# Score products in sets of three levels in a hybrid decoder step (GLA, HGRN2, convolution, pooling)

## The reference, cut to what matters

```python
h = _rmsnorm(x, norm_pre[l]); c = _split_cols(h @ w_in[l])
# groups A and C, per head of 64 channels, in blocks:
b = jnp.cumsum(gc, axis=2)
decay = jnp.exp(jnp.where(causal, b[:, :, :, None, :] - b[:, :, None, :, :], -jnp.inf))
scores = jnp.einsum('bhtd,bhsd,bhtsd->bhts', qc, kc, decay)
o = einsum('bhts,bhsv->bhtv', scores, vc) + einsum('bhtd,bhdv->bhtv', qc * jnp.exp(b), S)
S = exp(b_last)[..., None] * S + einsum('bhsd,bhsv->bhdv', kc * jnp.exp(b_last[:, :, None, :] - b), vc)
...
x = x + _rmsnorm(concatenate([o_a, o_b, o_c, o_d]) @ w_out[l], norm_post[l])
```

## Time and profile before

| what | value |
|---|---|
| median of 3 runs | 1050.87 us |
| span of the profiled execution, first to last instruction | 1048.4 us |
| what lies around the span (median less span) | 2.5 us |
| TensorE busy | 1005.1 us, 11780 matmuls |
| VectorE, ScalarE, GpSimd busy | 643.7, 434.0, 382.3 us |
| one tile of the loop, from a_k to the next a_k | 118.5 us |

### The profile page before, as it was taken

How to read it: one execution, slowest core, us unless ns; L and a number is a source line. 1 busy time by engine, 2 the same in 40 slices (tenths; PEclk the granted TensorE clock), 3 DMA queues, 4 the chain that set the end, 5 groups by cost and what they waited for, 6 DMA issues and landing times.

```text
span 1048.4 us, 27477 instructions
## 1 busy us (share of the span) xinstructions
PE 1005.1 (96%) x11780; PEld 749.1 (71%) x11780; DVE 643.7 (61%) x1356; ACT 434.0 (41%) x861; POOL 382.3 (36%) x526
## 2 busy tenths in 40 slices
PE   2998799999999999999999999999999999999997
PEld 2857477865887668865787668865787668866683
DVE  4997678645745567446745467446746477346564
ACT  6874444532534334432444334432434325233323
POOL 1434432174305640174304640164304650156300
PEclk9997699999999999999999999999999999999999
DMA  8720341001100011001100011001100011000011
GB/s 313 265 105 4 108 145 47 22 2 42 62 22 1 2 62 61 1 2 42 62 21 2 1 62 62 1 2 41 62 22 1 3 61 42 2 2 27 17 65 43
DMA packets 16187, 49.96 MB, mean 48 GB/s; under 512 B 2449, under 2 KB 3259, under 8 KB 16059
## 3 DMA queue, kind: packets, MB, share of 16 engines
q1 hardware_dynamic: 16067, 48.21, 13.2%
HBM read 38.44 MB, written 9.86 MB: 46 GB/s over the span
## 4 chain that ended last, share of the span: by engine, by line
PE 68%; DVE 21%; ACT 6%; issue 3%; DMA 1%; SPq 1%; POOL 0%; DVEq 0%; ACTq 0%
PE pj L676 30%; PE op L892 15%; PE pj L695 7%; PE sc L769 5%; DVE A L1896 4%; DVE w_lo L1789 2%; DVE X L2097 1%; DVE X L2090 1%; DVE X L2099 1%; PE op L738 1%; PE m L874 1%; PE m L826 1%; PE sc L912 1%; DVE A L1908 1%; PE op L912 1%
## 5 line engine op out<-in xcount | busy, mean ns | idle before, releaser
L676 PE MATMUL pj<-h_hi,w_hi 128*128 128x256 f16 (+1 forms) x1728 | 211.7, 266 | 1.0 <-DVE K L1840 0.5
L676 PE MATMUL pj<-h_lo,w_hi 128*128 128x256 f16 (+1 forms) x1728 | 210.2, 265 | 0.0
L676 PE MATMUL pj<-h_hi,w_lo 128*128 128x256 f16 (+1 forms) x1728 | 209.0, 264 | 0.0
L1896 DVE COPY_PREDICATED A<-cu,sc 64x128 f32<-64x128 uint8 x384 | 132.0, 344 | 114.3 <-PE sc L769 107.8
L501 POOL TENSOR_TENSOR G<-B 128x256 f32<-128x256 f32 x112 | 79.0, 705 | 294.5 <-DVE B L1831 171.2
L676 PEld LDWEIGHTS pj<-h_hi,w_hi 128*128 128x128 f16 x1728 | 152.3, 99 | 28.6 <-issue 4.4
L676 PEld LDWEIGHTS pj<-h_lo,w_hi 128*128 128x128 f16 x1728 | 158.7, 99 | 18.0
L676 PEld LDWEIGHTS pj<-h_hi,w_lo 128*128 128x128 f16 x1728 | 158.2, 99 | 17.5
L512 POOL TENSOR_TENSOR G<-G,Q 128x256 f32<-128x256 f32 x112 | 86.6, 773 | 117.4 <-issue 70.0
L1327 ACT ACTIVATE G<-G 128x512 f32<-128x512 f32 x112 | 69.1, 621 | 77.7 <-POOL G L502 77.6
L513 POOL TENSOR_TENSOR G<-G,K 128x256 f32<-128x256 f32 x112 | 92.6, 827 | 0.0
(11 more groups left out here) (284 smaller groups left out, 1402.2 us busy)
## 6 DMA issues: line engine op xcount, KB each, us to landing
xin<-in_x_prompt SPq DMA_DIRECT2D x17, 512.0 KB, 3.5
wo_hi<-in_w_units SPq DMA_DIRECT2D x16, 512.0 KB, 5.4
xres<-in_x_prompt SPq DMA_DIRECT2D x15, 512.0 KB, 3.6
out_y_prompt<-xres SPq DMA_DIRECT2D x14, 512.0 KB, 2.6
wo_lo<-in_w_units SPq DMA_DIRECT2D x12, 512.0 KB, 5.0
xres<-in_w_out SPq DMA_DIRECT2D x8, 256.0 KB, 3.2
gpost<-in_w_out SPq DMA_DIRECT2D x8, 256.0 KB, 4.2
m_hi<-in_state_gla SPq DMA_DIRECT2D x1, 512.0 KB, 8.5
```

The costliest lines, as they stand in the source:

```text
L676: m = pe.matmul(b[:, j * T:(j + 1) * T], w[:, k, col + 128 * j:col + 128 * j + 128], h[:, k, :], start=(n == 0 and k == 0), stop=(n == 2 a ...
L1896: m = dve.copy_predicated(out, mk.unsqueeze(1).broadcast_to([64, 4, 32 // h, h]), half(SC[hh], u)[:, 0:128].rearrange("p (q b w) -> p q b ...
```

## The change

1. From tile 2 on (`FIRST_SETS = 2`), the levels are grouped in `SETS`: 0 to 2, 3 to 5, and 6 with DIAG. The products of a set go to columns 0, 128 and 256 of SC and are issued one after the other; only the first of them waits for the copies of the set before. The copies wait for the last product of the set.
2. TensorE's list: six sets per tile in place of sixteen single products; `attend` and `updates` of a branch follow each other; both of branch 1 come after `b_b`; `recall(i, 1)` comes after `b_z`; `head_sums(i, 1)` between the halves of `c_z`.
3. GpSimd, ScalarE and VectorE get new orders; tile 8 uses the loop on these three, and on TensorE a list like that of the loop.
4. The fills of `pj` in tile 8 are in the order of the other tiles.

No computation is left out, and the number of instructions that compute stays the same.

```diff
+SETS = ((0, 1, 2), (3, 4, 5), (6, DIAG))
+FIRST_SETS = 2
...
+def set_of(i, lv):
+
+    if i < FIRST_SETS:
+        return (lv,)
+    return next(g for g in SETS if lv in g)
...
-            for i in range(2, NT):
+            for i in range(2, NT + 1):
                 for br in range(2):
-                    for lv in range(3):
+                    for lv in (0, 1, 2):
                         exponents(i, br, lv)
-                    factors(i, br, 0)
                     if br == 1:
                         key_product(i, 0)
-                    factors(i, br, 1)
-                    exponents(i, br, 3)
-                    for lv in range(2, 7):
+                    for lv in (0, 1, 2):
                         factors(i, br, lv)
-                        if lv < 5:
-                            exponents(i, br, lv + 2)
+                    for lv in (3, 4, 5):
+                        exponents(i, br, lv)
+                    for lv in (3, 4, 5):
+                        factors(i, br, lv)
                     key_exponents(i, br)
+                    exponents(i, br, 6)
+                    factors(i, br, 6)
                 key_product(i, 1)
...
         def scores(i, br, lv):
             T, NC, C = dims(i)
-            n = at_score(i, br, lv)
-            if n or i:
+            n, at_col = at_score(i, br, lv), CH * set_of(i, lv).index(lv)
+            if (n or i) and at_col == 0:
                 pe.wait_ge(*at("am", i, 2 * n))
...
-                                    col = (2 * c + j) * 32
+                                    col = at_col + (2 * c + j) * 32
...
+        def score_set(i, br, n):
+
+            for lv in SETS[n]:
+                scores(i, br, lv)
...
                 proj(i, "c_f")
                 proj(i, "a_q")
                 proj(i, "a_k")
-                values_proj(i, 0, (0,))
-                scores(i, 0, 0)
-                values_proj(i, 0, (1,))
-                scores(i, 0, 1)
+                values_proj(i, 0)
                 values_proj(i, 1, (0,))
-                scores(i, 0, 2)
+                score_set(i, 0, 0)
                 values_proj(i, 1, (1,))
-                scores(i, 0, 3)
-                proj(i, "c_q", (0,))
-                scores(i, 0, 4)
-                proj(i, "c_q", (1,))
-                scores(i, 0, 5)
+                proj(i, "c_q")
                 out_product(i - 1, 0, 0)
-                scores(i, 0, 6)
+                score_set(i, 0, 1)
                 out_product(i - 1, 0, 1)
-                scores(i, 0, DIAG)
                 proj(i, "d_v", (0,))
-                attend(i, 0)
+                score_set(i, 0, 2)
                 proj(i, "d_v", (1,))
                 transpose_keys(i, 0)
-                scores(i, 1, 0)
                 out_product(i - 1, 1, 0)
+                attend(i, 0)
                 updates(i, 0)
-                scores(i, 1, 1)
                 out_product(i - 1, 1, 1)
-                scores(i, 1, 2)
+                score_set(i, 1, 0)
                 recall(i, 0)
-                scores(i, 1, 3)
                 pool_product(i)
-                proj(i, "d_z", (0,))
-                scores(i, 1, 4)
-                proj(i, "d_z", (1,))
+                proj(i, "d_z")
                 head_sums(i, 0)
-                scores(i, 1, 5)
                 proj(i, "a_z", (0,))
-                scores(i, 1, 6)
+                score_set(i, 1, 1)
                 proj(i, "a_z", (1,))
-                if i < NT:
-                    transpose_x(i + 1, 0)
-                scores(i, 1, DIAG)
+                transpose_x(i + 1, 0)
                 proj(i, "b_c")
+                score_set(i, 1, 2)
+                proj(i, "b_v")
+                transpose_keys(i, 1)
+                transpose_x(i + 1, 1)
+                proj(i, "b_b")
                 attend(i, 1)
-                transpose_keys(i, 1)
-                proj(i, "b_v")
                 updates(i, 1)
...
-                proj(i, "b_b")
+                low_rank(i + 1)
+                proj(i, "b_z")
                 recall(i, 1)
...
+                log_alpha(i + 1)
+                proj(i, "c_z", (0,))
                 head_sums(i, 1)
-                proj(i, "c_z")
+                proj(i, "c_z", (1,))
...
         def copy_scores(i, br, lv):
             T, NC, C = dims(i)
-            n = at_score(i, br, lv)
+            n, at_col = at_score(i, br, lv), CH * set_of(i, lv).index(lv)
             for hh in range(2):
-                dve.wait_ge(*at("sc", i, 2 * n + hh + 1))
+                if at_col == 0:
+                    dve.wait_ge(*at("sc", i, 2 * at_score(i, br, set_of(i, lv)[-1]) + hh + 1))
+                else:
+                    dve.wait_ge(*at("am", i, 2 * n + hh - 1))
...
```

More of the change, by code:

```diff
@@ L79, in fill_order @@
     fills += [
-        (NT, "c_f"), (NT, "a_q"), (NT, "a_k"), (NT, "vi0"), (NT, "c_q"), (NT, "vi1"), (NT, "d_v"),
-        (NT, "d_z"), (NT, "po"), (NT, "a_z"), (NT, "b_c"), (NT, "b_v"), (NT, "b_b"), (NT, "tails"),
+        (NT, "c_f"), (NT, "a_q"), (NT, "a_k"), (NT, "vi0"), (NT, "vi1"), (NT, "c_q"), (NT, "d_v"),
+        (NT, "po"), (NT, "d_z"), (NT, "a_z"), (NT, "b_c"), (NT, "b_v"), (NT, "b_b"), (NT, "tails"),
         (NT, "b_z"), (NT, "c_z"),
@@ L1180, in _ @@
             out_section(0, 0)
+            attend(NT, 1)
             updates(NT, 1)
-            attend(NT, 1)
             tails_out(NT)
@@ L1915, in copy_scores, with copy_set @@
                 m.then_inc(*give(dve, "am", i, 2 * n + hh + 1))
+        def copy_set(i, br, n):
+            for lv in SETS[n]:
+                copy_scores(i, br, lv)
         def query_decay(i, br):
@@ L2355, in _ @@
                     x_scale(i + 1, 1)
+                copy_set(i, 1, 2)
+                query_decay(i, 1)
                 convolution(i)
-                states(i, 1, 0)
                 if i < NT:
@@ L2360, in _ @@
                 conv_out(i)
+                states(i, 1, 0)
                 states(i, 1, 1)
@@ L2365, in _ @@
                 gate_min(i, "B")
[L2366 removed]
                 gate(i, "B")
                 mix_lo(i, "B")
[L2369 to L2417 removed]
+                normalise(i, 1)
             gate_abs(NT, "C")
             gate_min(NT, "C")
[L2420 to L2421 removed]
             gate(NT, "C")
```

262 lines of the change are left out of this document (45 added, 217 removed).

## The result

| what | before | after |
|---|---|---|
| median of 4 runs | 1050.72 us | 1062.9 us |
| span of the profiled execution | 1048.4 us | 1061.3 us |
| mean granted clock of TensorE | 0.984 | 0.979 |
| TensorE, VectorE, ScalarE, GpSimd busy | 1005.1, 643.7, 434.0, 382.3 us | 992.4, 646.5, 428.7, 379.3 us |

A forecast was written before the change was run, and what follows sets the result against it. TensorE's border costs and few waits were taken to bound the kernel, with VectorE's slack deciding the sign. Per loop tile +4.7 - 3.3 = +1.45; six tiles +8.8, less 0.3, tile 8 -1.7: +6.8, 1057.7 us (range 1051 to 1063).

The forecast's parts named there:

- Part 1: TensorE's small products joined: 10 fewer runs per loop tile at 0.20 us, plus 0.1, so 2.1 us less work.
- Rivals 3 and 4: 3: matmuls beyond 32 in a run take 29 ns, 1077 us, chance 0.05; 4: joins save nothing, 1067 us, 0.03.
- Part 2: TensorE's waits before score 3, a_k, score 4 and `updates` go: 1.16 us less, leaving 115.2 us per tile.
- rival 1: TensorE's list, not the chain of VectorE and ScalarE, sets the time: 1029 us, chance 0.29.
- Part 3: New TensorE waits at the transposes of x, before `low_rank` and before a_k: +4.7 us per loop tile.
- Wait 1: TensorE waits for `x_scale` at the transposes of x, chunk 1: 2.8 us per tile.
- Wait 2: TensorE waits before `low_rank` for `x_lo` of chunk 1: 1.4 us per tile.
- wait 3: TensorE waits before a_k for `forget_in`: 0.55 us per tile.
- Tile 8: 20 runs become 9 (-2.2), the wait before a_k comes (+0.55), no next x to prepare: -1.7 us.
- Branch 0: Set factors ready 2.5 to 5 us before their products, so no wait; 0.2 us per tile if `transpose_keys` fails.
- Rival 2: The new waits bring TensorE's clock down: at worst 1.7 us per tile, six times, 1068 us, chance 0.04.
- The reasoning behind the sign: Faster or slower hangs on VectorE's slack where TensorE depends on it, 1.05 us at `x_scale`; slower 0.65.

The follow-up runs named there:

- the best version: Changed kernel with branch 1's two sets earlier on TensorE, their exponentials and copies earlier, normalise ahead of gate B: 1043.99 us, 0.9943 of the kernel before.
- Norm first: Changed kernel with `inv_rms` and `normalise` of branch 1 ahead of gate B's second half: 1060.14 us, 1.01 of the kernel before.
- early x_scale: Changed kernel with chunk 1's `x_norm` ahead of mix_hi A, `x_scale` ahead of gate A, `x_lo` ahead of the convolution: 1067.11 us, 1.0162 of the kernel before.
- all with a later set: Changed kernel with all reorderings so far, two copies ahead of gate_abs A, branch 1's set 3 in the middle of b_v: 1055.95 us, 1.0056.
- pool_out first: Changed kernel with `pool_out` ahead of `y_out` of the tile before on VectorE, in every tile: 1058.36 us, 1.0088 of the kernel before.

## Why the prediction was right, and where it was not

**Part 1 (fewer borders), right.** Two sets of 96 took 1.53 and 1.54 us to the next start, 16 ns per matmul; three times the 0.49 of the earlier trace rows and 0.11 for the way out of the tiling are 1.58. By the Trainium skill, "TensorE: Matmul & The Clock Gate", section "Back-to-back issue gap", 96 would have taken 2.4 us (an estimate from its 25 ns); the trace disagrees for small matmuls in four tiles of the array. Rivals 3 and 4 fall with the same rows.

**Part 2, right.** TensorE's own work is 114.85 us per tile, against 115.2. Whether a tile without any wait would run in it (rival 1) no run shows: the best version has 116.84 from a_k to a_k, with 1.54 idle.

**Part 3 (waits that come), the direction right, the sum too small.** 5.8 us per tile against 4.75:
- Before a_z: 1.28 against nothing. This is the step that failed. I asked who waits for `x_scale`, `x_lo` and `forget_in`, and not who waits for `pool_out`, which the change puts behind all copies of branch 1's first set and `y_out`. a_z is the second fill after `pool_product`, and `fill_order` shows it. I had the end of `pool_out` in my own walk (9.1 after recall for the step behind it) and never held it against the time at which TensorE asks for it, 8.1 after recall in this trace (632.66).
- Wait 1: 2.51 against 2.8. The chain took 31.7 and not 30.8. That 0.9 lies in small terms, mostly: `states` began 0.85 after recall, not 0.67; gate_abs D came at 9.45, not 9.1; the copies took 4.38, not 4.32, and gate D's first operation 0.97, not 0.69. The wait before a_z had taken 1.28 of it beforehand: together 3.79, 1.0 more than the 2.8.
- Wait 2: 1.23 against 1.4; wait 3: 0.79 against 0.55. Norm first shows this one to be separate from the others: 0.60 of it was won without touching them.

By a_k to a_k the tile is 120.65 against the forecast's 119.9. Two more terms lie beside it. Of the five tile distances three are 0.35 us longer than the others (120.66 and 121.0): two by the low clock, and the first, at full clock, as it is in the kernel before too (118.81 against 118.46). And the mean before was 118.53. So the loop gives 5 x 2.35 where the forecast has 1.45 a tile. Tile 8 was -1.65 from a_k to the end (130.39 to 128.74), as forecast. Branch 0, costed at nothing, shows no wait in tiles 3 to 7.

**Rival 2 (clock)** was worth 0.35 us in each of two tiles here, not 1.7 in each of six. Its 1.7 is right as a price: early x_scale pays 1.66 in four tiles and all with a later set 1.67 in five. What the forecast lacked is that it depends on the place of the wait: where another wait follows shortly, most of it is hidden.

**The reasoning behind the sign** held in a wider form than I wrote it. The forecast says that `x_scale` had 1.05 us of slack and lost it with TensorE's shorter stretch. The runs say that the kernel before had none, at `updates`, and that the change puts copies into the stretch from recall to `conv_out` (41.5 for 38.3 us), where all of the consumers are late together. The sum for wait 1 (30.8 less 28.1) does not use this slack, and so did not suffer from it. Before, the copies of levels 0 and 1 of branch 1 (2.5 us) were made before recall; a set can be copied only when its last level has run, and the first set was placed right before recall. It is that placement which costs, not the sets: with it mended, the same sets of three are 0.6% faster than the kernel before.

Why the gate's operations on VectorE take 0.69 us in one place and more in another (0.97 and up to 1.35 in the changed kernel, 1.8 in other orders) the traces tell in part. In the changed kernel GpSimd ran beside 22 of the 64 multiplications of the gates (L2000, L2002), and all 22 were longer; the 42 others all took 0.69. What the two engines share no run sets apart. Open is also why the same wait brings the clock down in one tile and not in the next.

## What to carry to other kernels

When work of one engine is joined into larger pieces, ask at once when the last operand of the piece is there and what its consumer stood ahead of: the engine that reads it gets its work later and in one block, and what the block is in front of is late. Measure the slack of a chain by padding it, in the kernel before too: the slack at the consumer that you happened to read is only an upper bound, and the tightest consumer may be another, here one on ScalarE. And if moving an instruction only changes who waits while the length of the stretch stays (41.5, 41.4), stop reordering within it and move work out of it. Look at the granted clock of each tile before a slower run is put down to the order: in two of these kernels the clock took most of what was lost, and a median over the whole run hides it.

## What was not expected of the hardware

- Waits of 2.3 to 4.7 us brought TensorE to its lower level, in some tiles and not in others. After 2.34 us it fell in two tiles of six (the transposes' row up to 1.78 in place of 1.09), after 3.03 with pool_out first in four, after 4.65 in all six. A wait of 2.38 to 2.39 before b_z did so in four tiles in one kernel and in five in another.
- The price was 0 to 0.35 us where another wait stood behind, 1.66 where none did, and up to 1.6 on top of the wait of 4.65: a wait can cost more than its length.
- The same four VectorE operations (128 x 128, f32 to f16) took 0.29 us each where GpSimd stood idle, and up to 1.10 where it ran.
- 96 small matmuls in four tiles of the array keep 16 ns from start to start; 32 keep 15.
